# Relative bias of a sparse attention: three bf16 parts in four 32-column tiles of TensorE, against two fp32r parts over the whole array

## The reference

```python
_, sel = lax.top_k(score, k_top)                      # score is causal
bias = rel_table[rel_bucket(posq[:, :, None] - take_rows(positions, sel))]
logits = jnp.einsum('bqhd,bqkd->bqhk', qb, k_sel).astype(jnp.float32) * A_HEAD_DIM ** -0.5
logits = logits + jnp.swapaxes(bias, 2, 3).astype(jnp.float32)
logits = jnp.where(valid[:, :, None, :], logits, NEG_INF)
p = jax.nn.softmax(logits, axis=-1).astype(v.dtype)
return jnp.einsum('bqhk,bqkd->bqhd', p, v_sel)
```

## Time and profile before

| | |
|---|---|
| runs | 3270.58, 3275.36, 3273.14 us, median 3273.14 |
| profiled execution, span on the core | 3269.0 us |
| PE / PEld / DVE / ACT / POOL busy | 93% / 76% / 48% / 19% / 35% of the span |
| sparse tiles, first to last `logits` product | 1981.5 to 2326.3 us in the span |
| mean granted clock of TensorE over the span | 0.95 of full |

### The profile page before, as it was taken

The page is one execution under the profiler, slowest core; times in us unless marked ns, Lnnn a source line. Parts: engine busy times, 40 slices in busy tenths (PEclk is TensorE's granted clock), DMA queues, the critical chain, the costliest instruction groups (busy, mean ns, idle before and its releaser), DMA issues.

```text
span 3269.0 us, 35251 instructions
## 1 busy us (share of the span) xinstructions
PE 3039.0 (93%) x14244; PEld 2470.3 (76%) x14244; DVE 1556.8 (48%) x1750; ACT 619.8 (19%) x970; POOL 1145.8 (35%) x527
## 2 busy tenths in 40 slices
PE   4999998699999999599989989999999999999997
PEld 3788876588888888468875768787778888888886
DVE  7752332733233334639997344544345333333337
ACT  3101121210000111321113643323202111111011
POOL 4533324644443444624331031000134444444341
PEclk6999998799999999779999988999999999999999
DMA  7431112011111111121221000000231111111111
GB/s 273 136 129 39 34 31 97 20 45 51 46 45 51 45 51 46 66 50 46 88 80 60 1 1 1 1 1 1 84 136 46 45 52 45 50 46 45 51 45 64
DMA packets 209033, 183.37 MB, mean 56 GB/s; under 512 B 19499, under 2 KB 194106, under 8 KB 208410
## 3 DMA queue, kind: packets, MB, share of 16 engines
q1 hardware_dynamic: 206618, 173.44, 17.0%
q10 hardware_dynamic: 2304, 8.39, 0.6%
HBM read 159.92 MB, written 20.97 MB: 55 GB/s over the span
## 4 chain that ended last, share of the span: by engine, by line
PE 78%; DVE 14%; POOL 2%; ACT 2%; issue 2%; DMA 1%; SPq 0%; DVEq 0%; POOLq 0%; ACTq 0%
PE PS L968 21%; PE PS L978 21%; PE PS L786 15%; DVE MB L1835 5%; PE PS L1102 4%; PE PS L1129 4%; PE PS L1173 3%; PE PS L772 2%; PE PS L1080 2%; POOL ACC L693 1%; DVE SQ L1603 1%; PE PS L1097 1%; PE PS L1013 1%; DVE MSUM L1559 1%; PE PS L1098 1%
## 5 line engine op out<-in xcount | busy, mean ns | idle before, releaser
L664 POOL TENSOR_TENSOR WHI<-RAW,ZERO 128x1024 fp32r<-128x1024 f32 x208 | 397.6, 1912 | 1729.0 <-PE PS L786 523.7
L666 POOL TENSOR_TENSOR WLO<-RAW,WHI 128x1024 fp32r<-128x1024 f32 x208 | 573.2, 2756 | 16.3
L786 PE MATMUL PS<-H,WHI 128*128 128x512 f32 x1088 | 338.9, 393 | 9.6 <-DVE L L1513 7.9
L786 PE MATMUL PS<-L,WHI 128*128 128x512 f32 x1088 | 336.4, 390 | 0.0
L786 PE MATMUL PS<-H,WLO 128*128 128x512 f32 x1088 | 335.7, 390 | 0.0
L1757 DVE TENSOR_TENSOR FT<-RL 128x1024 f32<-128x1024 f32 x64 | 120.9, 1889 | 424.2 <-ACT RL L1328 424.2
L1328 ACT ACTIVATE RL<-PS 128x1024 f32<-128x1024 f32 x64 | 65.7, 1027 | 1180.9 <-PE PS L968 1173.4
L786 PEld LDWEIGHTS PS<-H,WHI 128*128 128x128 f32 x1088 | 203.4, 189 | 52.3 <-issue 9.1
L1961 DVE TENSOR_REDUCE NMX<-PS 128x1 f32<-128x256 f32 (+7 forms) x128 | 97.0, 758 | 301.4 <-PE PS L1102 178.6
L786 PEld LDWEIGHTS PS<-L,WHI 128*128 128x128 f32 x1088 | 205.1, 188 | 43.1
L786 PEld LDWEIGHTS PS<-H,WLO 128*128 128x128 f32 x1088 | 204.8, 188 | 43.2
(11 more groups left out here) (292 smaller groups left out, 5501.2 us busy)
## 6 DMA issues: line engine op xcount, KB each, us to landing
RAW<-w_fc SPq DMA_DIRECT2D x64, 512.0 KB, 3.8
RAW<-w_ff SPq DMA_DIRECT2D x64, 512.0 KB, 3.8
RAW<-w_in SPq DMA_DIRECT2D x54, 512.0 KB, 3.9
ADA<-w_ada SPq DMA_DIRECT2D x32, 512.0 KB, 5.0
x_scratch<-X SPq DMA_DIRECT2D x2, 4096.0 KB, 13.7
RAW<-w_out SPq DMA_DIRECT2D x16, 512.0 KB, 4.1
X<-x_scratch SPq DMA_DIRECT2D x2, 4096.0 KB, 14.3
gate_scratch<-GST ACTq DMA_DIRECT2D x16, 512.0 KB, 2.6
```

The costliest lines, as they stand in the source:

```text
L664: nc.gpsimd.tensor_add(WHI[j][:, 0:n], RAW[j][:, 0:n], ZERO[:, 0:1].to_broadcast([P, n])).then_inc(s_whi, 1)
L666: nc.gpsimd.tensor_sub(WLO[j][:, 0:n], RAW[j][:, 0:n], WHI[j][:, 0:n].bitcast(F32)).then_inc(s_w, 1)
L786: last = mm(bank(b + t), wt[:, k, :], a[:, k * S + t * HALF:k * S + (t + 1) * HALF], start=(k == 0 and n == 0), stop=(k == KC - 1 and n == 2))
```

## The change

The bias's stationary operand shrinks from 128 columns to the 32 that aren't zero (`GROUP`: 8 heads times 4 queries), and each group's product writes only its own 32 rows of PSUM. For that the rows of a tile are reordered from (heads, 16 queries) to (group, heads, 4 queries): the constants `sel` and `reach`, the split of `AQP` by `STEPQ`, POOL's moves into `QS` and ACT's copies to `YA` follow. The operand is cut into three bf16 parts (`DPART`) in place of two fp32r parts, and `STEP` is bf16. So a chunk has 12 bias products of 128x32 weights in place of 8 of 128x128, and the bias products of both chunks come after the other products of both.

`KLO` lies on 128 rows (a fourth key copy on DVE), and L1097 uses all 128 rows. A sparse tile's logits, maximum and exponentials end at the last key that its 16 queries see, 128 b + 16 (r+1) with r = i % 8, in place of 128 (b+1). Since the transposes still read whole blocks of 128, POOL zeroes both `PB` buffers before the sparse tiles (each after the last dense tile's transposes from it), and ahead of the last `QS` moves; the exponentials of tiles 64 and 65 wait for it. `STEP` no longer lies over `AQP`, so `steps_of(1)` waits for no POOL work.

```diff
-        STEP = [region("STEP0", L0 + 1024, 4 * S, F32R), region("STEP1", X0, 4 * S, F32R)]
-        DHI = region("DHI", Y0 + 1536, NSTEP * P, F32R)
-        DLO = region("DLO", Y0 + 2048, NSTEP * P, F32R)
+        STEP = [region(f"STEP{j}", L0 + 1024 + 2048 * j, 2 * S, BF16) for j in range(2)]
+        DPART = [region(f"DPART{j}", Y0 + 1536 + 16 * j, 16, BF16) for j in range(3)]
...
+        def att_width(n):
+
+            b, r = ATT[n]
+            return P * (b + 1) if n < 64 else P * b + QT * (r + 1)
...
                     for tiles, i0, i1, moved in ((48, 0, 48, s_aq), (64, 48, 64, s_aq2)):
+                        if tiles == 64:
+                            pool.wait_ge(s_aq, 4)
+                            for j in range(2):
+                                pool.wait_ge(s_pt, 63 + j)
+                                nc.gpsimd.memset(PB[j][:, :], 0.0).then_inc(s_pbz, 1)
+                            pool.wait_ge(s_pbz, 2)
                         pool.wait_ge(s_lg, tiles)
-                        piece = lambda t, e: t[64 * e:64 * e + 64, :].rearrange("p (i n) -> p i n", n=64)[:, i0:i1]
-                        to = QS[:, :].rearrange("p (i e n) -> p i e n", e=2, n=64)[:, i0:i1]
+                        piece = lambda t, e: t[64 * e:64 * e + 64, :].rearrange("p (i n) -> p i n", n=16)[:, 4 * i0:4 * i1]
+                        to = QS[:, :].rearrange("p (i e n) -> p i e n", e=2, n=16)[:, 4 * i0:4 * i1]
...
             def logits(n):
                 b = ATT[n][0]
-                w = P * (b + 1)
+                w = att_width(n)
...
                         mm(dst[:, c:c + cw], QS[:, at], KHH[:, c:c + cw], start=True, stop=False)
-                        mm(dst[:, c:c + cw], QS[0:64, at], KLO[0:64, c:c + cw], start=False, stop=False)
+                        mm(dst[:, c:c + cw], QS[:, at], KLO[:, c:c + cw], start=False, stop=False)
                         mm(dst[:, c:c + cw], SELB[:, (i % NB) * P:(i % NB + 1) * P],
                            MB[:, MASK_AT[b] + c:MASK_AT[b] + c + cw], start=False, stop=False)
-                        for g in range(NSTEP):
-                            for part in (DHI, DLO):
-                                last = mm(dst[:, c:c + cw], part[:, g * P:(g + 1) * P],
-                                          STEP[i % 2][:, g * S + c:g * S + c + cw], start=False,
-                                          stop=(g == NSTEP - 1 and part is DLO))
+                    for c in range(0, w, HALF):
+                        cw = min(HALF, w - c)
+                        for part in range(3):
+                            for g in range(NSTEP):
+                                last = mm(dst[GROUP * g:GROUP * (g + 1), c:c + cw], DPART[part][:, :],
+                                          STEP[i % 2][:, g * S + c:g * S + c + cw], start=False, stop=(part == 2))
...
-                    src = bank(4, 2)[0:64, :].rearrange("p (r e c q) -> p r e c q", r=NB, c=4, e=2)
+                    src = bank(4, 2)[0:64, :].rearrange("p (j e c t) -> p j e c t", e=2, c=4, t=STEPQ)
                     for e in range(2):
-                        dst = YA[64 * e:64 * e + 64, :].rearrange("p (c b r q) -> p b r c q", c=4, b=NB, r=NB)[:, b]
+                        dst = YA[64 * e:64 * e + 64, :].rearrange("p (c b j t) -> p b j c t", c=4, b=NB, t=STEPQ)[:, b]
...
+                    if n in (64, 65):
+                        act.wait_ge(s_pbz, n - 63)
+                    w = att_width(n)
                     A(PB[n % 2][:, 0:w], bank(2 * (n % 2), 2)[:, 0:w], ACT.Exp, bias=NMX[:, n % 2:n % 2 + 1],
...
             def steps_of(i):
 
-                w = P * (i // NB + 1)
-                if i == 1:
-                    dve.wait_ge(s_aq2, 2)
+                w = att_width(64 + i)
...
+                    for part in range(2):
+                        link(V.tensor_copy(DPART[part][:, :], DF[:, :]))
+                        link(V.tensor_tensor(DF[:, :], DF[:, :], DPART[part][:, :], ALU.subtract))
+                    V.tensor_copy(DPART[2][:, :], DF[:, :]).then_inc(s_tpd, 1)
...
-                    V.tensor_sub(KLO[0:64, :], AKB[0:64, :], KHH[0:64, :].bitcast(F32)).then_inc(s_kparts, 1)
+                    for e in range(2):
+                        V.tensor_sub(KLO[64 * e:64 * e + 64, :], AKB[0:64, :], KHH[0:64, :].bitcast(F32)).then_inc(s_kparts, 1)
```

More of the change, by code:

```diff
@@ L41 @@
 NSTEP = QT // STEPQ
+GROUP = A_HEADS * STEPQ
 NEG = -1e30
@@ L117, in constants @@
     parts["rep"] = rep
-    reach = np.zeros((P, NSTEP, A_HEADS, QT))
-    for g in range(NSTEP):
-        for t in range(STEPQ):
-            reach[t * BUCKETS:(t + 1) * BUCKETS, g, :, g * STEPQ + t] = 1.0
-    parts["reach"] = reach.reshape(P, NSTEP * P)
+    reach = np.zeros((P, A_HEADS, STEPQ))
+    for t in range(STEPQ):
+        reach[t * BUCKETS:(t + 1) * BUCKETS, :, t] = 1.0
+    parts["reach"] = reach.reshape(P, A_HEADS * STEPQ)
     parts["tri"] = np.where(i[None, :] > i[:, None], NEG, 0.0)
@@ L266, in build @@
         POSB = region("POSB", Y0 + 512, S)
-        STEP = [region("STEP0", L0 + 1024, 4 * S, F32R), region("STEP1", X0, 4 * S, F32R)]
-        DHI = region("DHI", Y0 + 1536, NSTEP * P, F32R)
-        DLO = region("DLO", Y0 + 2048, NSTEP * P, F32R)
+        STEP = [region(f"STEP{j}", L0 + 1024 + 2048 * j, 2 * S, BF16) for j in range(2)]
+        DPART = [region(f"DPART{j}", Y0 + 1536 + 16 * j, 16, BF16) for j in range(3)]
         SELB = region("SELB", Y0 + 2560, 512, BF16)
         THR = region("THR", Y0 + 3072, 256)
-        DF = region("DF", Y0 + 3328, NSTEP * P)
+        DF = region("DF", Y0 + 3328, GROUP)
         YA = region("YA", K0 + 8192, 4 * S)
         SEL = region("SEL", K0 + 8192, NB * P)
-        REACHED = region("REACHED", K0 + 9216, NSTEP * P)
+        REACHED = region("REACHED", K0 + 9216, GROUP)
         REP = region("REP", K0 + 13328, P)
@@ L368, in build @@
         s_tab, s_tp = sem("bias_table_in"), sem("bias_steps_product")
-        s_step = sem("steps")
+        s_step, s_pbz = sem("steps"), sem("probability_tails_zeroed")
         s_g = [sem(f"gates_in{j}") for j in range(4)]
@@ L1383, in _ @@
                     c = (c0 - AQ) // P
-                    read_tile(w, [(AQP[:, :].rearrange("p (i c q) -> p c i q", c=4, q=QT)[:, c], every,
-                                   {"scale": float(A_DIM) ** -0.5, "split": QT})])
+                    read_tile(w, [(AQP[:, :].rearrange("p (j c t) -> p c j t", c=4, t=STEPQ)[:, c], every,
+                                   {"scale": float(A_DIM) ** -0.5, "split": STEPQ})])
                 elif kind == "cq":
@@ L1937, in _ @@
                         link(V.tensor_scalar(THR[rows, :], POSB[rows, t:S:STEPQ], steps[rows, :], None, ALU.subtract))
-                    for g in range(NSTEP):
-                        at = slice(g * P, (g + 1) * P)
-                        view = lambda t: t.rearrange("p (e c q) -> p e c q", e=2, q=QT)
-                        link(V.tensor_tensor(view(DF[:, at]), view(REACHED[:, at]),
-                                             DLT[:, :].rearrange("p (c e o) -> p e c o", e=2, o=1).broadcast_to([P, 2, 4, QT]),
-                                             ALU.mult))
-                    link(V.tensor_copy(DHI[:, :], DF[:, :]))
-                    V.tensor_sub(DLO[:, :], DF[:, :], DHI[:, :].bitcast(F32)).then_inc(s_tpd, 1)
+                    view = lambda t: t[:, :].rearrange("p (e c t) -> p e c t", e=2, t=STEPQ)
+                    link(V.tensor_tensor(view(DF), view(REACHED),
+                                         DLT[:, :].rearrange("p (c e o) -> p e c o", e=2, o=1).broadcast_to([P, 2, 4, STEPQ]),
+                                         ALU.mult))
+                    for part in range(2):
+                        link(V.tensor_copy(DPART[part][:, :], DF[:, :]))
+                        link(V.tensor_tensor(DF[:, :], DF[:, :], DPART[part][:, :], ALU.subtract))
+                    V.tensor_copy(DPART[2][:, :], DF[:, :]).then_inc(s_tpd, 1)
                 if n == KEYS_AT:
@@ L1957, in _ @@
                 dve.wait_ge(s_lg, n + 1)
-                w = P * (ATT[n][0] + 1)
+                w = att_width(n)
                 if n >= 2:
```

10 lines of the change are left out of this document (4 added, 6 removed).

## The result

The changed kernel takes 3149.7 us (median of four runs, 3147.9 to 3152.7) against 3271.9 us of the kernel before (four runs, 3268.0 to 3275.4): ratio 0.9632, interval 0.9620 to 0.9643. It is 122 us faster.

The account below looks back on a forecast made before the run. PE alone was taken to set the pace in the sparse tiles. Savings of 84.4 us (blocks 1 to 7) plus 12 (block 0) less 1.2 (keys) made 95.2, giving 3178 us, range 3160 to 3200.

Parts of the forecast that it names:

- The overlap of the four groups: Bias products on PE: four groups stream at once, so three parts of 512 columns cost 0.69 us, not 1.84.
- DVE as a cover: Sparse tiles: DVE's 3.93 us in a block 7 tile stays under PE's new 5.61, so DVE is not the bound.
- the pace of the bf16 steps: DVE's step operations with bf16 output stay at their pace, 0.68 us a step.
- the fourth key copy: DVE's added key operation, for which PE stands idle, adds 1.2 us to the path.
- ACT's finer pattern as free: ACT's two copies per block cost no more with the finer pattern; if it doubled them, 10 us.
- no overlap: Rival: the four groups' products run one after another, 12 streams in place of 8, about 3307 us; chance 0.09.
- a pair costs 0.115 us: Rival: each pair of weight load and 32-column product costs 0.115 us, not 0.05, giving 3247 us; chance 0.10.
- the price of a pair: Least cost on PE of a weight load and product with 32 weight columns: taken as 0.05 us, from below 0.029.
- my own sum for blocks 1 to 7: Blocks 1 to 7 priced at eight tiles plus 2.1 us each, saving together 84.4 us.
- the change of shape: PE going to 32-column tiles and back, once per tile: 2 x 0.19 = 0.38 us.
- block 0: First eight sparse tiles: tile 65's steps no longer wait for POOL; 12 us saved (9 to 17).
- The rival of the clock: Rival: PE's clock stays at half through block 2, 25 us less gain, 3203 us; chance 0.12.

Follow-up runs that it names:

- pieces of 32: The changed kernel with the bias products cut to pieces of at most 32 columns: 3389.8 us, ratio 1.0368.
- the run with the wait back: The changed kernel, but the steps of tile 65 wait again until POOL has read its last queries: 3163.1 us, ratio 0.9676.
- full columns: The changed kernel with its three bf16 parts on 128 columns of weights again, no 32-column tiles: 3264.9 us, ratio 0.9988.
- two parts: The changed kernel without its third bf16 part, the bias left less exact: 3139.9 us, ratio 0.9600.
- keys early: The changed kernel with the keys' DVE operations and first steps at n = 40, not 52, and KLO and STEP buffers moved: 3131.5 us, ratio 0.9584.

## Why the prediction was wrong, step by step

**The overlap of the four groups** carried the prediction, and it held: 108 us of stage time hang on it. The tile time of block 7 came out near: 5.61 us were forecast for its mean width of 968 columns; the tile of 960 took 5.24, and 5.55 to 5.63 only those of 992 to 1024. DVE as a cover, the pace of the bf16 steps, the fourth key copy (PE's pause for the keys is 14.3 us where it was 13.1, so +1.2), ACT's finer pattern as free (0.59 us a copy, as before): all as forecast. The rival *no overlap* is refuted, and so is *a pair costs 0.115 us*.

**The step that failed is the price of a pair**, "I take 0.05", with "from below: a quarter of the 0.115 of 128 columns, 0.029". Measured: at or under 0.014 in twelves with a change of shape in it, and 0.008 in the rows of the pieces of 32. The lower bound was not one: the 0.115 was a price of fp32r weights of 128 columns loaded one after another, and nothing says that four loads of 32 columns come one after another too. In this kernel four start within 15 ns. With 0.015 in place of 0.05 my own sum for blocks 1 to 7 falls by 10.6 us (230.2 to 219.6), most of it in blocks 1, 4 and 5, whose chunks are narrow.

**The second term that was mis-sized is the change of shape**, 0.38 us per tile. The profile after shows 0.22 to 0.24 per tile, one more trip costs 0.31, and `KLO`'s 0.29 per chunk. At 0.22 the sum falls by a further 9.0, to 210.6 us; measured were 209.3 (203.7 and an eighth interval of 5.65). The 0.43 of the earlier trace rows was read rightly: a product of 512 columns there would be followed after 0.23, so the way out of the 64-row shape costs 0.20. The 0.41 was not: it is the distance behind a chunk's first product, and in the kernel after `KLO` follows `KHH` after 0.32 us with no change of shape between them. I had taken a streak's 0.23 as what it would be.

**The third is block 0**, 12 us against 20.9. The chain of causes was right: no wait for tile 65, POOL's moves later, two tiles' steps held up beside them. But 12 us meant that tile 72's exponential comes at 2009.4, 12.9 us after the end of POOL's moves; it came at 2000.4, 5.9 us after their end. 2.0 of the 9.0 us are POOL's, which was done at 1994.5 and not at 1996.5. The other 7.0 are the tiles behind it: I had taken 1.60 us each at the full clock and 2.7 at half, and nearly all of them at half, and they took 0.96 and 1.10 at the full clock and 1.7 to 1.8 at half, to which it fell only at about 1997. With a pair at 0.015 and the shapes at 0.22, my own sum gives 1.02 in place of 1.60, so this term failed by the same two prices, and by the clock. The stall of PE for the steps was 1.23 us and not 2 to 4. That the freed wait is what saves the block, the run with the wait back shows: 15 us.

The three make 10.6 + 9.0 + 8.9 = 28.5 of the 27.7 us between forecast and measured. That they meet so well is in part luck: my sum counts an eighth interval of block 7 (2.8 us of the 22.3), which the time does not show, since what follows the last exponential is no shorter after (942.0 us against 941.4), and it takes off 1.2 us for the keys, which tile 63's time does not show either, with the clock moving by as much.

**By parts, in the stage:** the key part on 128 rows 28 us, the steps' wait 15 (as it costs in the changed kernel), the ends at the last key 10, and the bias products in 32-column tiles the rest, some 70 of 123.5, by difference and not by a run of its own; of these, one part alone (full columns) would give back 108, since three parts in full columns are dearer than the two before.

**The rival of the clock** did not decide here, but it was not idle: in the changed kernel block 1 began with 6.6 us at half clock, and at two parts block 1 ran at half clock throughout. It stays open what exactly makes the clock rise earlier or later at the same work: tile 63 came between 1976.9 and 1988.6 us among kernels that are the same up to there but for small edits (keys early aside).

## What to carry to other kernels

Products with few weight columns that write different sets of 32 PSUM rows can run side by side at next to no price per pair, even in pieces of 128 columns and in either order of the loops; down to that size, count streams, not instructions. In pieces of 32 PE paused for reasons that the profile doesn't show, and the kernel was slower than before the change. Bound a price from below only by something that must be serial. And price an idle stretch of PE with the half clock behind it: a wait of 10 us cost 15, and a pause of 14 us (DVE's key copies beside POOL) was a matter of moving four operations ahead.

## What the runs showed of the hardware that I had not expected

Sets of 32 columns keep their own pace: with a set's three products in a row, weight loads still came four at a time every 0.21 us and the time was the same (3151.6 against 3149.7). Twelve pairs of 32 columns and 16 streamed columns took 0.17 us, 0.014 a pair, with the change of shape behind them; in pieces of 32 columns 202 of them started within 1.63 us, 0.008 each, and then PE paused 2.51. A trip from 128x128 to 32-column tiles and back cost 0.22 to 0.31 us, and one to a 64-row product and back 0.29, of which 0.09 were the way in and 0.20 the way out. DVE's copies of fp32 data stretch to the end of POOL's operations beside them: the same second copy of 64x1024 took 0.69 us alone (keys early) and 5.68 beside POOL, where the first took 3.50. The first ends at 1928.86, 0.55 us after POOL's L769 (1914.83 + 13.48 = 1928.31), and the second at 1934.57, 0.55 us after the first of the two operations that the row of L773 holds (1934.02), in these rows of the kernel after, in the timelines of DVE and POOL:

```profile
1925.36 3.50 DVE L1961 CAST KHH<-AKB 64x1024 fp32r<-64x1024 f32 x1
1928.89 5.68 DVE L1962 CAST KHH<-AKB 64x1024 fp32r<-64x1024 f32 x1
...
1914.83 13.48 POOL L769 TENSOR_TENSOR QS<-AQP,AQH 64x3072 fp32r<-64x3072 f32 x2 [80.81 <-PE PS L1093]
1928.38 11.35 POOL L773 TENSOR_TENSOR QS<-AQH,ZERO 64x3072 fp32r<-64x3072 f32 x2
```
